# Seven decay levels of a recurrent branch: matmuls with 64 moving columns in place of 128, and masked copies of 512 elements in place of 1024

## What is computed

```python
b = jnp.cumsum(lfc, axis=2)                         # log decays, summed along the chunk
diff = b[:, :, :, None, :] - b[:, :, None, :, :]
decay = jnp.exp(jnp.where(causal[None, None, :, :, None], diff, NEG_BIG))
attn = jnp.einsum('bhtk,bhsk,bhtsk->bhts', qc, kc, decay)
o_intra = jnp.einsum('bhts,bhsv->bhtv', attn, vc)
```

## Time and profile before

| | us |
|---|---|
| median of 3 runs | 1185.15 (1182.85 to 1188.54) |
| the profiled execution, its own time | 1184.03 |
| its span, from the first to the last instruction | 1181.9 |
| mean granted clock of TensorE, as a share of 2.4 GHz | 0.976 |
| PE busy, of the span | 1118.4 |
| PEld busy | 1012.1 |
| DVE busy | 806.0 |
| ACT busy | 672.6 |

### The profile page before, as it was taken

How to read it: one execution, slowest core, us unless ns; L and a number is a source line. 1 busy time by engine, 2 the same in 40 slices (tenths; PEclk the granted TensorE clock), 3 DMA queues, 4 the chain that set the end, 5 groups by cost and what they waited for, 6 DMA issues and landing times.

```text
span 1181.9 us, 19911 instructions
## 1 busy us (share of the span) xinstructions
PE 1118.4 (95%) x7376; PEld 1012.1 (86%) x7376; DVE 806.0 (68%) x1229; ACT 672.6 (57%) x1113; POOL 54.5 (5%) x64
## 2 busy tenths in 40 slices
PE   3999898998999999999999997999898999999998
PEld 3899797988998888998888896887778998888998
DVE  3788797535778777667877766444645778777666
ACT  3546756467465655556656444465747566565553
POOL 0000000000420000120000010000000220000010
PEclk8999999999999999999999998998979999999999
DMA  5244433334555554564554454333213555554563
GB/s 211 91 152 161 143 128 128 106 108 143 179 179 179 211 177 147 196 208 166 209 180 180 158 189 149 143 131 119 88 56 108 179 183 209 180 196 163 178 216 107
DMA packets 31995, 187.09 MB, mean 158 GB/s; under 512 B 4032, under 2 KB 7488, under 8 KB 14144
## 3 DMA queue, kind: packets, MB, share of 16 engines
q1 hardware_dynamic: 31936, 186.28, 44.9%
HBM read 184.43 MB, written 1.05 MB: 157 GB/s over the span
## 4 chain that ended last, share of the span: by engine, by line
PE 81%; DVE 9%; ACT 6%; issue 3%; POOL 1%; DMA 1%; SPq 0%; DVEq 0%; POOLq 0%; ACTq 0%
PE acc L591 73%; PE area_a L591 4%; PE area_t L591 3%; DVE wlo L1444 2%; ACT whi L1072 1%; ACT L1072 1%; ACT he L1072 1%; POOL mixed L2020 1%; DMA raw<-in_w_projT_a 1%; PE area_t L847 1%; ACT gates L1072 0%; DVE xr L1614 0%; DVE s_after L1984 0%; DVE score L1681 0%; DVE st L1633 0%
## 5 line engine op out<-in xcount | busy, mean ns | idle before, releaser
L591 PE MATMUL acc<-hs,whi 128*128 128x256 f32 (+1 forms) x2528 | 641.6, 335 | 16.9 <-DVEq L1453 7.8
L591 PE MATMUL acc<-hs,wlo 128*128 128x256 f32 x1792 | 488.9, 284 | 0.0
L591 PEld LDWEIGHTS acc<-hs,whi 128*128 128x128 f32 x2528 | 428.0, 194 | 59.6 <-DVEq L1453 12.0
L1072 ACT ACTIVATE whi<-raw 128x1024 fp32r<-128x1024 f32 (+2 forms) x378 | 351.6, 980 | 84.2 <-PE acc L591 66.5
L1444 DVE TENSOR_TENSOR wlo<-raw,whi 128x1024 fp32r<-128x1024 f32 (+3 forms) x258 | 271.3, 1094 | 145.9 <-ACT whi L1072 145.5
L591 PEld LDWEIGHTS acc<-hs,wlo 128*128 128x128 f32 x1792 | 344.2, 192 | 10.9
L591 PE MATMUL acc<-hid,whi 128*128 128x512 f32 (+1 forms) x660 | 185.6, 350 | 1.1 <-DVE wlo L1444 1.1
L591 PE MATMUL acc<-hid,wlo 128*128 128x256 f32 x528 | 145.5, 281 | 0.0
L1533 DVE TENSOR_TENSOR wlo<-raw,whi 128x1024 fp32r<-128x1024 f32 x120 | 141.7, 1222 | 3.9
L591 PEld LDWEIGHTS acc<-hid,whi 128*128 128x128 f32 x660 | 113.9, 188 | 18.3 <-DVE wlo L1444 1.5
L591 PEld LDWEIGHTS acc<-hid,wlo 128*128 128x128 f32 x528 | 99.4, 188 | 1.5
(11 more groups left out here) (313 smaller groups left out, 1153.8 us busy)
## 6 DMA issues: line engine op xcount, KB each, us to landing
raw<-in_w_gu SPq DMA_DIRECT2D x66, 1024.0 KB, 4.8
raw<-in_w_dn SPq DMA_DIRECT2D x48, 704.0 KB, 4.1
raw<-in_w_up SPq DMA_DIRECT2D x10, 1024.0 KB, 4.8
raw<-in_w_gates1b SPq DMA_DIRECT2D x8, 1024.0 KB, 4.8
raw<-in_w_out SPq DMA_DIRECT2D x8, 1024.0 KB, 4.8
raw<-in_w_qk SPq DMA_DIRECT2D x8, 1024.0 KB, 4.7
raw<-in_w_gates SPq DMA_DIRECT2D x8, 1024.0 KB, 4.8
raw<-in_w_projT_b SPq DMA_DIRECT2D x7, 1024.0 KB, 4.8
```

The source lines that it names most:

```text
L591: return nc.tensor.matmul(out, w, m, start=start, stop=stop, skip_group_check=True)
L1072: return nc.scalar.activation(out, in_, f, **kw)
```

## The change

Levels 1 to 7 change in two places; level 0, the exponents, the exponentials, the multiplications, the masks' values, the order of work and every wait stay. On PE the weights are still the 128 columns of a group, and the moving operand is now only its 64 columns of second halves: for half size 1 every second column, for 64 the last 64 columns as one run. The products are packed without gaps into the first 512 columns of `area_t`, one bank. On DVE the copy covers 8 x 64 = 512 elements: the mask and `h0` are read and written at the columns of second halves only, the products from the packed 512 columns. The build of the changed kernel has the same number of instructions on every engine and in the same order.

```diff
                         if lv == 0:
-                            w, m_ = hk[:, at_], flat(bq)[:, at_]
-                        else:
-                            w = m_ = he[lv % 2][:, at_]
-                        m = mm(o[:, h, queries(tt)], w, m_, True, True)
+                            m = mm(o[:, h, queries(tt)], hk[:, at_], flat(bq)[:, at_], True, True)
+                            continue
+                        w = he[lv % 2][:, at_]
+                        later = w.rearrange("p (n s h) -> p n s h", s=2, h=LEVELS[lv])[:, :, 1, :]
+                        m = mm(flat(o)[:, 64 * (2 * h + tt):64 * (2 * h + tt) + 64], w, later, True, True)
...
-                    m = con[:, C_LEV + P * lv:C_LEV + P * (lv + 1)].bitcast(I32).unsqueeze(1)
-                    out = h0[:, :, :].rearrange("p h (t n) -> p (h t) n", n=P)
-                    src = (area_a if in_a else area_t)[:, :, :].rearrange("p h (t n) -> p (h t) n", n=P)
-                    v.copy_predicated(out, m.to_broadcast([P, 8, P]), src)\
-                        .then_inc(S("a_freed" if in_a else "t_freed"), 1)
+                    m = con[:, C_LEV + P * lv:C_LEV + P * (lv + 1)].bitcast(I32)
+                    out = flat(h0[:, :, :])
+                    src = flat((area_a if in_a else area_t)[:, :, :])
+                    if lv == 0:
+                        m = m.unsqueeze(1).to_broadcast([P, 8, P])
+                        out, src = (w.rearrange("p (a n) -> p a n", n=P) for w in (out, src))
+                    else:
+                        half = LEVELS[lv]
+                        n = P // (2 * half)
+                        m = m.rearrange("p (n s h) -> p n s h", s=2, h=half)[:, :, 1, :]
+                        m = m.unsqueeze(1).to_broadcast([P, 8, n, half])
+                        out = out.rearrange("p (a n s h) -> p a n s h", n=n, s=2, h=half)[:, :, :, 1, :]
+                        src = src[:, 0:512].rearrange("p (a n h) -> p a n h", n=n, h=half)
+                    v.copy_predicated(out, m, src).then_inc(S("a_freed" if in_a else "t_freed"), 1)
```

## The result

| | before | after |
|---|---|---|
| median of 20 runs, us | 1183.99 (1180.96 to 1188.54) | 1187.9 (1185.53 to 1191.36) |
| ratio to before, 95% interval | | 1.003, 1.002 to 1.0041 |
| the profiled execution, its own time | 1184.03 | 1185.53 |
| its span | 1181.9 | 1183.7 |
| mean granted clock of the profiled execution | 0.976 | 0.973 |

What follows compares the result with a forecast made beforehand. PE was taken as the bound, busy 95% of the span and 81% of the chain. 0 for PE and 0.53 us for one copy, taken from the median 1185.15, gave 1184.6 us; range 1181.0 to 1187.3 us.

Steps and rivals of the forecast that it cites:

- PE's matmuls: Matmuls of levels 1 to 7: weight loads keep instructions 0.11 us apart with 64 moving columns, so a gain of 0.
- the rival: Level matmuls: streaming sets the distance, 0.06 us (56 ns by the skill's rule); 3.9 us less with the copy, 1181.3; chance 0.10.
- The copies: DVE's seven masked copies: 0.53 us less each over 512 elements, 3.7 us in all, short runs adding nothing.
- the 0.80 taken: Length in us forecast for a 512-element copy, if all it costs above another PSUM-reading instruction is fixed.
- the 0.67 that was the other end: Length in us of a 512-element copy if its extra cost is in proportion, 0.66 less than now.
- The exponents' rows: DVE's exponents in runs of 1 to 64 elements all last 691 to 694 ns, taken to show run length doesn't matter.
- The place where it counts: Of the seven shorter copies, only level 6's was to shorten the kernel, by 0.53 us; the others nothing.
- level 6: Its copy at 226.11 us is on the chain; all 0.53 us come earlier, worth 0.5 us, then PE is late.
- Level 7: Its shorter copy gives nothing back, since PE is in its stream of weight tiles and does not wait.
- the sum: Whole kernel: 0 for PE and 0.53 us for one copy taken off the total, median 1184.6 us, 0.05% less.
- The clock rival: In the levels the array does less, so one more low-clock stretch costs 1.7 us, giving 1186.3 us; chance 0.06.

## Why the prediction was wrong

**PE's matmuls: right.** The instructions of a level start 0.11 us apart with 64 moving columns as with 128, where the rival had 0.06. The 1.73 us for 1.79 are no gain: the tile behind the level takes 5.80 us for 5.75, and from the start of level 1 to the start of the next step on PE it is 7.5 us in both. The chain before, then after:

```profile
159.44 1.79 PE area_t L591 x16
161.22 5.75 PE acc L591 x48
166.97 0.89 PE area_a L591 x8
```
```profile
156.66 1.73 PE area_t L591 x16
158.40 5.80 PE acc L591 x48
164.20 0.89 PE area_a L591 x8
```

All these matmuls, and those of the earlier trace rows, have 128 weight columns, whose load the prediction prices at 110 ns; no run had fewer weight columns at so few moving ones. The Trainium skill (TensorE: Matmul & The Clock Gate, Back-to-back issue gap) calls the formula from which the rival's 56 ns came that of an isolated matmul, and says that in a stream of loads and matmuls both set the spacing. The trace agrees with the latter, 0.11 us.

**The copies: right in size for long runs, wrong that runs don't matter.** DVE's timeline, levels 1, 2, 3 and 6:

```profile
159.39 1.32 DVE L1857 COPY_PREDICATED h<-con,area_t 128x512 f32<-128x512 int32 x1
...
168.86 1.31 DVE L1857 COPY_PREDICATED h<-con,area_t 128x512 f32<-128x512 int32 x1
...
175.34 0.68 DVE L1857 COPY_PREDICATED h<-con,area_t 128x512 f32<-128x512 int32 x1
...
223.20 0.74 DVE L1857 COPY_PREDICATED h<-con,area_t 128x512 f32<-128x512 int32 x1
```

Levels 1 and 2, with runs of one and two elements, gained nothing at all; the others last 0.68 to 0.75, below the 0.80 taken and near the 0.67 that was the other end. The exponents' rows at the same run lengths were the wrong neighbour: another instruction, and no PSUM in it (which of the two matters was not tried). It cost nothing here: from the first matmul of the stretch to level 5 PE takes 64.0 us after for 64.1 before. All seven save 3.1 us, not 3.7.

**The place where it counts: right for level 6, and one place missed.** Level 6 gave 0.6 us, and PE became the bound there. Level 7 was said to give nothing back, because PE is in its stream. But the transposes of the attention's probabilities write `area_t`, so they wait for that copy. Before (first) PE's last matmul of the tile had started at 236.39, and the transposes started 0.15 us behind the end of the copy; after (second) they no longer wait for it:

```profile
235.27 1.34 DVE L1846 COPY_PREDICATED h<-con,area_t 128x1024 f32<-128x1024 int32 x1
...
236.76 0.63 PE L847 MATMUL area_t<-con,m_p 128*128 128x128 f32 x4
```
```profile
231.84 0.75 DVE L1857 COPY_PREDICATED h<-con,area_t 128x512 f32<-128x512 int32 x1
...
233.08 0.60 PE L847 MATMUL area_t<-con,m_p 128*128 128x128 f32 x4
```

That is worth 0.3 us. Both gains, 0.9 us together, are in the traces of all six kernels with the short copies, and in none of the six without. The rest of the 1.5 us, some 0.5, arises between 320 and 371 us, far behind the edit. That stretch takes either 51.1 or 50.7 us: the shorter time is in five of the six kernels with the short copies, but also in the kernel before with 2.1 us of added work, and the change with fourteen added matmuls has the longer one. So it can't be put down to the edit, and its cause stays open.

**The step that failed is the sum.** It took the 0.53 us gained at 227 us off the end of the kernel, and put everything behind the levels at nothing, as if every later stage took as long wherever it starts. No row was given for that. One stage does not: PE is idle for 5.13 us in front of it, the granted clock falls in that wait, and how long it stays down depends on where the stage stands against the clock's changes. The stage took 26.15 us in place of 20.78: 1 us sooner cost 5 us. That 0.53 should have been 0.9 is the smaller error, and of the other sign.

**The clock rival: the right resource in the wrong place.** I looked for it in the levels, because the array does less there; the clock from 157 to 190 us is 1.00 after as before. Its price, 1.7 us for one more stretch, was too small by a factor of three, and its chance of 0.06 with it. The page of before has a sign of the stage: its clock row has an 8 in the slice from 709 to 739 us, the first behind the start, next to a 5 us wait that I did not look at, since nothing was edited there. The row has such digits in the attention steps too, from 798 us on, and there the changed trace has about the same clock.

**Why it is not just noise.** If the work stood anywhere against the clock's changes, by chance in each execution, the medians would not move by 4 us and back with added work. In the eight traces of the table above, the start of the levels' stretch lies 48.0 to 48.6 us ahead of the same fall of the clock near 192 us, although that start itself varies between 142.6 and 146.0: in the four traces with the latest start the clock's first stretch at the lower level, near 23 us, lasts 6.8 us, in the other four 3.4. So by the time of the levels the work and the clock's changes stand in a fixed relation. What ties them was not tried, and there is one trace of each kernel: how much the place varies from one execution to the next is seen only in the spread of the runs, 1185.53 to 1191.36 us for the change.

## What to carry to other kernels

A microsecond gained ahead of a stage in which TensorE waits and the clock falls is not a microsecond at the end: here it came back as minus five. Look at every idle time of TensorE behind the edit, and at the granted clock after it, not only at the edited stretch; and before blaming or praising an edit of this size, add its shift as useless work to the old kernel. The remedy that worked here is to keep TensorE busy in the long wait: five unread matmuls took 3.4 us off the old kernel (by the ratio), while more of them in short waits gave nothing. The Trainium skill (TensorE: Matmul & The Clock Gate, HAM oscillation) advises for another case, waits for DMA between short groups of matmuls, to order the loops so that TensorE stays busy.

## What the runs showed of the hardware

- Matmul instructions with 128 weight columns of 4 bytes start 0.11 us apart at 2.4 GHz with 8, 64, 128 or 136 moving columns; with 8 it is 0.21 us at 1.2 GHz.
- A `copy_predicated` from PSUM lasts 1.33 us over 1024 elements and 0.68 to 0.75 over 512, but 1.31 over 512 in runs of one or two elements, both from packed products and, in the kernel with the copies alone, from strided ones (1.32 and 1.31 there too).
- The same instructions from the first matmul of `w_fvl` on took 17.4 us at full clock, and 18.9, 19.1, 20.8, 24.3, 26.2 or 27.9 us by where they stood against the changes of the clock.
- Waits of the same length did not cost the same: behind the 5.1 us wait near 720 us the clock stayed low for 6.8 to 27.3 us, behind the waits of 4.2 us near 190 and of 3.0 us near 279 for 3.4 us in each of the eight traces of the table.
